# Three attentions of a one-core layer program: copies and value products one step later, four score buffers used in place, three buffers of turned tiles

## The reference

```python
s = jnp.einsum('ngrbqd,ngbkd->ngrbqk', qb, kb).astype(jnp.float32) * (HEAD_DIM ** -0.5)
s = s - slopes.reshape(g, r)[None, :, :, None, None, None] * (diff * dist_scale).astype(jnp.float32)
s = jnp.where(mask, s, NEG_INF)
lse = jax.nn.logsumexp(s, axis=-1)
p = jnp.exp(s - lse[..., None])
o = jnp.einsum('ngrbqk,ngbkd->ngrbqd', p.astype(v.dtype), vb)
...
return gates[..., 0:1] * o_cmp + gates[..., 1:2] * o_slc + gates[..., 2:3] * o_win
```

## Time and profile before

| | |
|---|---|
| Time, median of 3 runs | 3399.21 us (3398.13 to 3400.4) |
| The profiled execution's own time | 3400.3 us |
| Its span in the profile | 3398.5 us |
| PE busy | 3280.4 us, 97% of the span |
| DVE, ACT, POOL busy | 47%, 35%, 43% |
| NSA attention (us from the span's start) | 215 to 298 |
| Dilated attention | 361 to 396 |
| Sliding-window attention | 1528 to 1604 |

### The profile page before, as it was taken

The page is one execution under the profiler, slowest core; times in us unless marked ns, Lnnn a source line. Parts: engine busy times, 40 slices in busy tenths (PEclk is TensorE's granted clock), DMA queues, the critical chain, the costliest instruction groups (busy, mean ns, idle before and its releaser), DMA issues.

```text
span 3398.5 us, 42789 instructions
## 1 busy us (share of the span) xinstructions
PE 3280.4 (97%) x15192; PEld 2656.3 (78%) x15192; DVE 1590.7 (47%) x2709; ACT 1200.3 (35%) x1869; POOL 1465.6 (43%) x715
## 2 busy tenths in 40 slices
PE   7999899999989999999999999999999999899998
PEld 5876678887767888877788878787888887688886
DVE  2244535521216556458665432566556453752223
ACT  3245433322234432236533243114432232653322
POOL 3440254445414544451644454445544454054442
PEclk9969999999989999999999999999999999999999
DMA  4310045543212555320355423202555322022332
GB/s 148 93 56 1 11 145 194 200 150 93 81 38 81 186 196 203 101 85 14 124 202 193 165 89 99 62 26 81 185 191 205 101 93 87 1 86 93 99 99 68
DMA packets 103106, 376.11 MB, mean 111 GB/s; under 512 B 11456, under 2 KB 11584, under 8 KB 102848
## 3 DMA queue, kind: packets, MB, share of 16 engines
q1 hardware_dynamic: 102816, 373.86, 33.2%
q0 software_dynamic: 160, 0.52, 0.1%
HBM read 372.24 MB, written 2.10 MB: 110 GB/s over the span
## 4 chain that ended last, share of the span: by engine, by line
PE 84%; DVE 3%; issue 1%; ACT 1%; POOL 0%; DVEq 0%; ACTq 0%; POOLq 0%
PE bank L722 20%; PE bank L723 20%; PE bank L724 20%; PE bank L813 2%; PE bank L808 2%; PE bank L809 2%; PE bank L1262 2%; PE bank L766 1%; PE bank L767 1%; PE bank L768 1%; PE bank L954 1%; PE bank L1158 1%; PE bank L903 1%; PE bank L974 1%; PE bank L1159 1%
## 5 line engine op out<-in xcount | busy, mean ns | idle before, releaser
L604 POOL TENSOR_TENSOR w_lo<-raw,w_hi 128x1024 fp32r<-128x1024 f32 x501 | 1222.4, 2445 | 1437.6 <-ACT w_hi L1341 1437.6
L1341 ACT ACTIVATE w_hi<-raw 128x1024 fp32r<-128x1024 f32 x501 | 526.9, 1058 | 1204.7 <-PE bank L724 1016.8
L722 PE MATMUL bank<-h_hi,w_hi 128*128 128x512 f32 x2264 | 883.8, 390 | 0.0
L723 PE MATMUL bank<-h_lo,w_hi 128*128 128x512 f32 x2264 | 881.6, 389 | 0.0
L724 PE MATMUL bank<-h_hi,w_lo 128*128 128x512 f32 x2264 | 881.5, 389 | 0.0
L722 PEld LDWEIGHTS bank<-h_hi,w_hi 128*128 128x128 f32 x2264 | 425.5, 188 | 90.9 <-issue 2.6
L723 PEld LDWEIGHTS bank<-h_lo,w_hi 128*128 128x128 f32 x2264 | 425.4, 188 | 88.9 <-issue 1.0
L724 PEld LDWEIGHTS bank<-h_hi,w_lo 128*128 128x128 f32 x2264 | 425.4, 188 | 88.7
L2438 DVE CUSTOM_DVE_ANT_0 ada_raw<-ada_raw,cond_row 128x1024 f32<-128x1024 f32 x192 | 310.7, 1622 | 277.6 <-DMA ada_raw<-ada 268.7
L722 PE MATMUL bank<-hid_hi,w_hi 128*128 128x512 f32 x880 | 344.0, 391 | 0.0
L724 PE MATMUL bank<-hid_hi,w_lo 128*128 128x512 f32 x880 | 342.4, 389 | 0.0
(11 more groups left out here) (362 smaller groups left out, 4135.4 us busy)
## 6 DMA issues: line engine op xcount, KB each, us to landing
raw<-weights SPq DMA_DIRECT2D x501, 512.0 KB, 3.5
ada_raw<-ada SPq DMA_DIRECT2D x192, 512.0 KB, 4.3
layer_const<-layer_const SPq DMA_DIRECT2D x5, 512.0 KB, 3.8
x<-x_t SPq DMA_DIRECT2D x1, 2048.0 KB, 7.6
cond_row<-cond SPq DMA_DIRECT2D x4, 512.0 KB, 4.3
y_t<-x SPq DMA_DIRECT2D x8, 256.0 KB, 2.0
tables<-big_const SPq DMA_DIRECT2D x1, 768.0 KB, 7.4
cols<-columns SPq DMA_DIRECT2D x1, 569.5 KB, 8.6
```

The source lines that it names most:

```text
L604: nc.gpsimd.tensor_tensor(w_lo[k % RING][:, :, :], raw[k % RING][:, :, :], w_hi[k % RING][:, :, :].bitcast(F32), ALU.subtract).then_inc(sm ...
L722: mm(out, w_hi[r][:, at, :], hi, start=first and at == 0, stop=False)
L723: mm(out, w_hi[r][:, at, :], lo, start=False, stop=False)
L1341: fn(w_hi[t % RING][:, :, :], raw[t % RING][:, :, :], ACT.Copy).then_inc(sm.hi_done, 1)
```

## The change

At step s, after the change:

- PE: scores of job s; turn of job s-2; value product of job s-4.
- ACT: exponential of job s; copy of the turned tiles of job s-2.
- DVE: minimum of job s; inverse and norm of job s-1; output of job s-5.

`s` and `p` become one set of four buffers. In the first part the exponential writes over its input; in the late one the two stand side by side in one row, so that the sink's column stays. `pt` has three buffers. The statistics move to `ln_small`. The minimum of job s now waits for the turn of s-4 and no longer for the exponential of s-2; the exponential waits for the turn of s-4 and no longer for that of s-2. Each loop is one step longer, and the work in between is moved by up to two steps.

```diff
+            whole = place(f"att_p_{name}", [P, 4, 520], F32, at)
+            p0 = 0 if name == "first" else 260
...
+                s=[whole[:, r, 0:520 - p0] for r in range(4)], p=[whole[:, r, p0:520] for r in range(4)],
+                pt=[place(f"att_pt_{name}{r}", [P, S], F32, (at + 2080, at + 2592, more)[r]) for r in range(3)])
...
-                for step in range(len(jobs) + 3):
+                for step in range(len(jobs) + 4):
-                    if step >= 3:
-                        j, it = step - 3, jobs[step - 3]
+                    if step >= 4:
+                        j, it = step - 4, jobs[step - 4]
                         pe.wait_ge(sm.att_copied, a + j + 1)
...
-                    elif step == 14:
+                    elif step == 16:
                         group_sum("first", items, 6)
-                    elif step >= 17:
-                        pe.wait_ge(sm.att_out, n["att_g"] + step - 4)
-                        out_spread("first", items, step - 17)
+                    elif step >= 18:
+                        pe.wait_ge(sm.att_out, n["att_g"] + step - 5)
+                        out_spread("first", items, step - 18)
...
-                for step in range(len(jobs) + 1):
+                for step in range(len(jobs) + 2):
-                        wait(act, sm.att_turned, a + j - 1)
+                        wait(act, sm.att_turned, a + j - 3)
-                    if step >= 1:
-                        j, it = step - 1, jobs[step - 1]
+                    if step >= 2:
+                        j, it = step - 2, jobs[step - 2]
                         act.wait_ge(sm.att_turned, a + j + 1)
-                        wait(act, sm.att_pv, a + j - 1)
+                        wait(act, sm.att_pv, a + j - 2)
...
-                for step in range(len(jobs) + 4):
+                for step in range(len(jobs) + 5):
-                        wait(dve, sm.att_exp, a + j - 1)
+                        wait(dve, sm.att_turned, a + j - 3)
-                            v.tensor_copy(s[:, 2 * P:2 * P + 1], sink)
+                            v.tensor_copy(bufs["sink"][j % 2], sink.unsqueeze(2).to_broadcast([P, 2, 1]))
-                    if step >= 4 and jobs[step - 4]["last"]:
-                        j, it = step - 4, jobs[step - 4]
+                    if step >= 5 and jobs[step - 5]["last"]:
+                        j, it = step - 5, jobs[step - 5]
```

More of the change, by code:

```diff
@@ L270, in program @@
         AT = {}
-        for name, at in (("first", s1), ("late", big + 13312)):
+        for name, at, more in (("first", s1, h_at + 5 * S), ("late", big + 13312, big + 13312 + 3104)):
+            whole = place(f"att_p_{name}", [P, 4, 520], F32, at)
+            p0 = 0 if name == "first" else 260
             AT[name] = dict(
-                s=[place(f"att_s_{name}{r}", [P, 520], F32, at + r * 520) for r in range(2)],
-                p=[place(f"att_p_{name}{r}", [P, 520], F32, at + 1040 + r * 520) for r in range(2)],
-                pt=[place(f"att_pt_{name}{r}", [P, S], F32, at + 2080 + r * S) for r in range(2)])
+                s=[whole[:, r, 0:520 - p0] for r in range(4)], p=[whole[:, r, p0:520] for r in range(4)],
+                sink=[whole[:, e:4:2, 2 * P:2 * P + 1] for e in range(2)],
+                pt=[place(f"att_pt_{name}{r}", [P, S], F32, (at + 2080, at + 2592, more)[r]) for r in range(3)])
         bias = place("bias", [P, 4, S], F32, s1 + 3104)
@@ L340, in program @@
         kcmp = small[:, 48:80]
-        att_min = [small[:, 144 + r:145 + r] for r in range(2)]
-        att_sum = [small[:, 146 + r:147 + r] for r in range(2)]
-        att_inv = [small[:, 148 + r:149 + r] for r in range(2)]
+        att_min = [ln_small[:, 0, r:r + 1] for r in range(4)]
+        att_sum = [ln_small[:, 1, r:r + 1] for r in range(4)]
+        att_inv = [ln_small[:, 2, r:r + 1] for r in range(4)]
         lam = small[:, 150:151]
@@ L961, in attention @@
                         for t, (_, keys) in enumerate(it["v"]):
-                            op = turn(bank[2 + j % 2][0:keys, t * P:(t + 1) * P], bufs["p"][j % 2][:, at:at + keys],
+                            op = turn(bank[2 + j % 2][0:keys, t * P:(t + 1) * P], bufs["p"][j % 4][:, at:at + keys],
                                       ident)
@@ L973, in attention @@
                         for t, (v, keys) in enumerate(it["v"]):
-                            op = mm(out, v, bufs["pt"][j % 2][0:keys, t * P:(t + 1) * P],
+                            op = mm(out, v, bufs["pt"][j % 3][0:keys, t * P:(t + 1) * P],
                                     start=it["first"] and t == 0, stop=it["last"] and t == len(it["v"]) - 1)
@@ L1576, in between @@
                         group_squares("first", items, step // 2)
-                    elif step == 12:
+                    elif step == 13:
                         act.wait_ge(sm.att_out, TT * NSA_HEADS + 8)
                         group_squares("first", items, 6)
-                    elif step == 15:
+                    elif step == 16:
                         group_root("first", items, 0)
@@ L2150, in between @@
                         group_widen("first", items, 1)
-                    elif step == 18:
+                    elif step == 19:
                         group_norm(items, 0, NORM_SPREAD["first"])
```

15 lines of the change are left out of this document (7 added, 8 removed).

## The result

| | before | after |
|---|---|---|
| Median of 20 runs, us | 3398.2 (3393.38 to 3402.8) | 3403.55 (3398.97 to 3406.02) |
| Ratio of the times, 95% interval | | 1.0016 (1.0009 to 1.0023) |
| The profiled execution's own time, us | 3400.3 | 3404.5 |
| Its span, us | 3398.5 | 3402.7 |

The changed kernel is slower by 5.4 us between the medians, 3 to 8 us by the interval.

A forecast was written before the change was run, and what follows sets the result against it. The prediction took PE, 97% busy, and its ring with DVE in the attentions as the bound, with ACT not waited for. Terms 0 + 0 + 0 + 0.6 + 0.64 + 0.3 + 0 gave +1.5 us, so 3400.7 us, range 3394 to 3405.

The forecast's parts named there:

- rival 2: NSA: moving DVE's output costs its copy in rounds where DVE is late; 2.3 to 4.6 us plus 0.9, chance 0.14.
- Rival 1: Attentions: ACT's chain binds after all and deeper buffers free PE's turns; -11 us, 3388, chance 0.08.
- rival 3: NSA's first pair: PE's slow-clock stretch changes; 3 to 4 us saved or some 8 lost, chance 0.10.
- Copies a step later, four buffers: Attentions: the ring through ACT, 1.95 us, lies below PE and DVE's 2.37, so lengthening it gives 0.
- the rule on repeating gaps: PE's turns: a repeating gap can mean too few buffers; 22 us and 3377 by that rule, not believed.
- Value products later: Attentions: PE's products run a step later with the same sum of work; 0, in NSA -3 to +3 us.
- DVE's output in another step: NSA: output moves to the step with the compressed branch's norm; +0.6 us, between 0 and 4.6.
- End of NSA: After NSA's last turn: one more idle product, +0.64 us; moved short and wide products even, at worst +0.9.
- End of the sliding window: Behind the sliding window's last turn: two value products come before the last one; +0.3 us.
- End of the dilated attention: End of dilated attention: earlier last scores and root against one more value product; 0, between -0.8 and +0.7 us.

The follow-up runs named there:

- g3: Kernel before with new buffers, new order in dilated and sliding-window attentions only, sink copied by two one-column copies: 3397.77 us, ratio 0.9994.
- e1: The kernel before run and profiled once more, no edit: 3398.67 us, ratio 1.0002.
- f1: The changed kernel with the sink copied by two copies of one column each instead of one of two columns: 3401.92 us, ratio 1.0007 to before.
- e3: Kernel before with the new buffers, statistics and waits, and the new order of steps in NSA alone: 3400.5 us, ratio 1.0007.
- e2: Kernel before with the new buffers, statistics and waits, but the old order of steps everywhere: 3403.07 us, ratio 1.0013.
- g2: Kernel before with new buffers, statistics and waits, old order everywhere, sink copied by two copies of one column each: 3400.85 us, ratio 1.0006.
- e4: Kernel before with new buffers, statistics and waits, new order in dilated and sliding-window attentions, old order in NSA: 3401.41 us, ratio 1.0005.
- f2: Kernel before with one edit, the sink's copy writing two columns instead of one: 3402.19 us, ratio 1.0012.
- g1: Kernel before with one edit, the sink's copy writing three columns instead of one: 3402.03 us, ratio 1.0011.

## Why the prediction was right or wrong

The time, 3403.55 us, lies in the range, and no difference above 0.2% was forecast and none came. That later copies and deeper buffers give nothing was read rightly. But that the time lies in the range is in part luck: the likeliest value was 2.9 us low, and the difference to before was +5.4 us where the sum said +1.5. The range was wide for the sake of rival 2 and the near halves of 1 and 3. Rivals 1 and 2 fell; what filled it were a copy that has no term and slow stretches that rival 3 didn't name. By its steps:

- **Copies a step later, four buffers: 0.** Right. The inner 48 window jobs took 53.29 and 53.30 us, and the wait moved to the exponential as foretold. That PE's gap names a result and no buffer decided it: the rule on repeating gaps, by which 22 us were to be had, gave nothing. Rival 1 fell.
- **Value products later, and DVE's output in another step: 0 and +0.6.** The second pair's minima took 32.77 for 32.87 us: 0 for the first, and nothing seen of the second. Of the first pair, whose rounds of i = 0 were to pay half of it, the clock hides more than 0.3 us. Rival 2, at least 2.3 us, would have shown about half of it in the second pair, and fell.
- **End of NSA: +0.64.** The step mis-sized. It measured +1.49: 0.66 for the idle product, and some 0.8 for the short and the wide product that now stand behind the last scores. These were counted at even, on the ground that the last scores and turns would come as much sooner. The last scores came only 0.2 us sooner, and the last turn 0.3 us later.

The end of NSA in the timeline of after, which answers to the earlier trace rows:

```profile
290.06 1.13 PE L955 MATMUL bank<-key_rows,proj 128*128 128x512 f32 x2
...
292.63 0.66 PE L963 MATMUL bank<-kept,att_p_first 128*128 128x128 f32 x4 [0.45 <-DVE att_p_first L2026]
...
294.55 0.48 PE L975 MATMUL bank<-att_pt_first,vcmp 31*128 31x128 f32 x2
294.96 0.91 PE L860 MATMUL bank<-kept 128*128 128x384 f32 x2
295.71 1.05 PE L975 MATMUL bank<-att_pt_first,v_slc 128*128 128x128 f32 x8
296.60 0.81 PE L860 MATMUL bank<-kept 128*128 128x384 f32 x2
297.25 1.05 PE L975 MATMUL bank<-att_pt_first,v_win 128*128 128x128 f32 x8
298.14 0.81 PE L860 MATMUL bank<-kept 128*128 128x384 f32 x2
```
The last scores stand 290.06 - 258.45 = 31.61 us behind the minimum of job 24 (31.81 before), and the last turn but one 292.63 - 258.45 = 34.18 us (34.28 before). That turn waits 0.45 us for DVE's norm in both kernels, and the norm comes by way of DVE's minimum from the last scores. Behind it PE now has a wide product where it had the short one, and behind the last turn the short product and the idle one come on top: the last turn, at 294.02, is 35.57 us behind that minimum (35.28 before), and from it to the stick-breaking part 4.86 us pass for 3.67. The "at worst +0.9" beside the term was nearly the truth.

- **End of the sliding window: +0.3.** Too high. From first scores to projection the window took 77.04 us with the new order and single copies (g3), 77.10 with the old (e1): 0. The end itself did grow, by half of the term: from the last turn to the projection 2.82 us pass in after and f1, 2.66 and 2.67 in before and e1. It was made good at the start, where the ring gets under way: from the first minimum to the ninth 10.65 us pass in f1 and g3, 10.94 in e1. The prediction has no term for the start.
- **End of the dilated attention: 0, between -0.8 and +0.7.** It measured about -0.7, near the lower bound (35.4 to 36.0 us in the five kernels with the new order, 36.2 to 36.7 in eight with the old, e3 left out). The root came sooner, as argued. In after, the last scores start at 386.76 and the table load at 390.48:

```profile
386.76 1.02 PE L955 MATMUL bank<-key_rows,proj 128*128 128x512 f32 x2
...
390.33 0.95 PE L905 MATMUL bank<-kept,sq 128*128 128x2 f32 x8
390.48 1.28 ACT L1458 ACT_TABLE_LOAD   x1
```
That is 3.7 us, where it was 3.8, but both starts are 0.9 us sooner. The prediction's 2.1 to 2.3 us for turn, product and sum add up to 2.0 to 2.1, which changes nothing.

- **What had no term at all: the sink's copy.** The diff changed it from one column to two, the prediction went past it, and with what goes with it behind the window it is the largest single cost: 1.2 us at the window's start, of which 0.7 are left at its end, and some 3.4 us in all. Five pairs of kernels differ in that copy alone: after and f1, e2 and g2, e4 and g3, f2 and before, g1 and before. The wider copy has the higher ratio in each, by 0.0009, 0.0007, 0.0011, 0.0012 and 0.0011, in the mean 0.0010, or 3.4 us, by the intervals an estimate good to some 2 us. Only the intervals of the last two leave out no difference; that all five point one way is what carries the figure. The mean granted clock of the runs points the same way: it is lower with the wide copy in all five, by 0.0004 to 0.0019, in the mean 0.0011, which at 2.5 us for 0.001 is an estimated 2.7 us of the 3.4.
- **The rest is the clock, in stretches that rival 3 didn't name.** It looked at NSA's first pair. That one's clock did leave 0.73, for 0.79, but the kernel before itself had 0.83 in e1, so nothing beyond the spread of one program is seen. (Its price of 8 us for a slow clock through the whole second pair was mis-sized: by its own rows, 11.3 us lost in 24 of slow clock, it is some 29.) The stretches 127 and 495 us behind the window's first minimum are in the profiles of all six kernels with the wide copy and in none of the eight others. f2 and g1, which differ from before in that copy alone, have them too. So the copy brings them, as far as one profile of each kernel can show; why 1.2 us at the window's start do it, and 1.3 or 2.6 us in NSA don't, stays open. A third stretch, 710 us ahead of the window (the first row of the windows above), is in all six kernels that have the new order in NSA or in the dilated attention, and in none of the eight others. With it the leg ahead of the window is 0.3 to 0.8 us longer than in e1. What in the order brings it stays open. So does why e3 and e4, with the same two stretches as after, lack another one some 710 us behind the window's start and end their last leg 3 us sooner; before has that one in one of its two profiles and lacks it in the other.

Put together, from legs of after against those of e1, which has the like clock ahead of the window, and without the first pair of NSA: NSA +1.5, dilated -0.7, ahead of the window +0.7, window +0.7, behind it +3.4, in all +5.6 for the 5.4 measured. Against the legs of the first profile of before the sum is 5.6 as well. It adds up one profile of each kernel, whose runs differ by 2 us and more among themselves, so its closeness says little.

## What to carry to other kernels

A wait that moves from one instruction to the next on the same engine is no gain; ask who waits for that engine. In a diff, cost each operation whose shape changes, even one of two columns: where DVE copies within SBUF, look in the timeline at what GpSimd runs at that place. At the end of a loop that is made one step longer, price every product that is put off, and take off only what the trace shows to come sooner: in NSA 0.8 us of 1.3 were paid. And where slow stretches of the clock come and go between two profiles of one program, one profile per kernel is too few to price an edit of 1 us.

## What the runs showed of the hardware

- A DVE copy of one column took 0.15 us beside a GpSimd piece of 2.35 us; one of two or three columns took 1.32 to 1.33 us, until that piece was over, with no wait in any view (before, f1, after, f2, g1).
- In a kernel with PE 97% busy the granted clock still differs from run to run, 0.974 to 0.977 in 97 of 100 runs of before, and the time with it, some 2.5 us for each 0.001. Small edits change which short stretches are slow, hundreds of us away from the edit, and that was worth as much here as all that the edit did at its own place.
